# Four row pairs in a chain per feed-forward stage, and one weight sum of each pair made by accumulating DMAs

## What is computed

```
def swiglu(x, w13, w2):
    gate, up = jnp.split(x @ w13, 2, axis=-1)
    return (jax.nn.silu(gate) * up) @ w2
...
for i in range(DEPTH):
    x = layer_norm(ALPHA * x + 0.5 * swiglu(x, ffn1_w13[i], ffn1_w2[i]), ln_g[i, 0], ln_b[i, 0])
    ...
    x = layer_norm(ALPHA * x + 0.5 * swiglu(x, ffn2_w13[i], ffn2_w2[i]), ln_g[i, 2], ln_b[i, 2])
```

## Time and profile before

| | |
|---|---|
| median of 3 runs | 2465.41 us (2463.21 to 2465.69) |
| profiled execution | 2466.14 us, its span 2464.2 us |
| TensorE busy | 98% of the span, granted clock 0.996 |
| VectorE, ScalarE, GpSimd busy | 75%, 54%, 17% |
| HBM read | 414.92 MB, 169 GB/s over the span |

### The profile page before, as it was taken

One profiled execution on the slowest core, in us unless ns is written; L12 is line 12 of the kernel. 1 busy time (PEld: TensorE's weight loads), 2 busy tenths in 40 slices (PEclk: granted clock), 3 DMA queues, 4 the chain that ended last, 5 costly groups with the idle time before them and its releaser, 6 DMA issues. The chain is left out here.

```text
span 2464.2 us, 32871 instructions
## 1 busy us (share of the span) xinstructions
PE 2410.9 (98%) x13023; PEld 2027.1 (82%) x13023; DVE 1852.3 (75%) x2384; ACT 1319.6 (54%) x1637; POOL 409.4 (17%) x463
## 2 busy tenths in 40 slices
PE   9999999999999999999989999999999998999999
PEld 7888878888888888888878888888878876998998
DVE  5466679889875798898768888887675667897554
ACT  5444555555664556556556655664553355444442
POOL 0002310000001100000230000001359602580000
PEclk9999999999999999999999999999999999999999
DMA  8555445656554465565515565565445542336553
GB/s 273 188 187 156 143 146 190 204 171 200 193 172 137 137 197 196 177 199 188 167 58 184 188 209 171 187 206 158 133 149 191 189 153 71 116 124 205 171 188 111
DMA packets 313945, 418.10 MB, mean 170 GB/s; under 512 B 18761, under 2 KB 271042, under 8 KB 313794
## 3 DMA queue, kind: packets, MB, share of 16 engines
q1 hardware_dynamic: 313794, 416.01, 51.8%
HBM read 414.92 MB, written 1.05 MB: 169 GB/s over the span
## 5 line engine op out<-in xcount | busy, mean ns | idle before, releaser
L536 DVE TENSOR_TENSOR wlo<-raw,whi 128x2048 fp32r<-128x2048 f32 (+1 forms) x370 | 861.4, 2341 | 159.0 <-ACT whi L529 158.2
L529 ACT ACTIVATE whi<-raw 128x2048 fp32r<-128x2048 f32 (+1 forms) x375 | 700.4, 1887 | 6.0 <-DMA raw<-in_ffn_w_dram 3.1
L695 PE MATMUL ps<-whi,xh 128*128 128x512 f32 (+2 forms) x1367 | 510.8, 374 | 7.9 <-DVE wlo L1647 2.2
L697 PE MATMUL ps<-whi,xl 128*128 128x512 f32 (+2 forms) x1367 | 503.5, 368 | 0.0
L696 PE MATMUL ps<-wlo,xh 128*128 128x512 f32 (+2 forms) x1367 | 503.1, 368 | 0.0
L695 PE MATMUL ps<-whi,oh 128*128 128x512 f32 x944 | 380.1, 403 | 0.0
L697 PE MATMUL ps<-whi,ol 128*128 128x512 f32 x944 | 369.0, 391 | 0.0
L696 PE MATMUL ps<-wlo,oh 128*128 128x512 f32 x944 | 367.9, 390 | 0.0
L695 PEld LDWEIGHTS ps<-whi,xh 128*128 128x128 f32 x1367 | 258.0, 189 | 56.8 <-issue 11.9
L697 PEld LDWEIGHTS ps<-whi,xl 128*128 128x128 f32 x1367 | 257.9, 189 | 43.2
L696 PEld LDWEIGHTS ps<-wlo,xh 128*128 128x128 f32 x1367 | 258.2, 189 | 41.0
(11 more groups left out here) (412 smaller groups left out, 3988.8 us busy)
## 6 DMA issues: line engine op xcount, KB each, us to landing
raw<-in_ffn_w_dram SPq DMA_DIRECT2D x350, 512.0 KB, 4.9
raw<-in_ffn_w_dram SPq DMA_DIRECT2D x88, 1024.0 KB, 5.0
raw<-in_w_ff_dram SPq DMA_DIRECT2D x32, 1024.0 KB, 5.4
raw<-in_w_out_dram SPq DMA_DIRECT2D x20, 1024.0 KB, 4.9
raw<-in_w_in_dram SPq DMA_DIRECT2D x20, 1024.0 KB, 5.1
raw<-in_dsa_w_in_dram SPq DMA_DIRECT2D x32, 512.0 KB, 4.6
raw<-in_dsa_w_in_dram SPq DMA_DIRECT2D x12, 1024.0 KB, 5.1
raw<-in_fox_w_in_dram SPq DMA_DIRECT2D x16, 512.0 KB, 5.0
```

The lines of the kernel that those rows point to most:

```text
L529: act.activation(hi(u)[:, 0:w], raw[:, (slot[u] + 1) % SLOTS, 0:w], ACT.Copy).then_inc(sem("hi_ready"), n)
L536: dve.tensor_tensor(lo(u)[:, 0:w], raw[:, (slot[u] + 1) % SLOTS, 0:w], hi(u)[:, 0:w].bitcast(F32), ALU.subtract).then_inc(sem("lo_ready"), n)
L695: pe.matmul(o, ah, bh, start=start, stop=False, skip_group_check=True)
L697: return pe.matmul(o, al, bh, start=False, stop=stop, skip_group_check=True)
```

## The change

- `PAIRED` is (3, 5, 7, 9) and not (3, 6, 9): the stage has plain units 0, 1 and 2 and then four pairs, one behind the other.
- Where a pair follows a pair, the first two sums, their parts and the down splits are interleaved at the end of `paired`, in a new order on VectorE and ScalarE (`two_summed`, `three_summed`).
- The third form's sum is taken from VectorE. GpSimd issues two DMAs of 512 KB each that add the weights of unit v + 2, read from DRAM, onto raw(v + 1) in SBUF, once unit v + 1 has landed and form_1 is made. ScalarE's high part of the third form waits for both.
- In the last pair of a stage, VectorE splits one unit and not two ahead of the last `gated_low`.
- Room for descriptors of GpSimd's DMAs grows from 512 to 2048 bytes per partition; to make room, `cum`, `kr` and `rope_m` share the space of `BT`, which is used much later.

```diff
-PAIRED = (3, 6, 9)
+PAIRED = (3, 5, 7, 9)
...
+                if kind == "ffn":
+                    A, D = ffn_units(st)
+                    for n, q in enumerate(st["pairs"]):
+                        v = A(q + 1)
+                        dst = raw_of(v + 1).rearrange("p (k h c) -> p k h c", k=4, h=2)
+                        landed(pool, v + 1)
+                        pool.wait_ge(sem("form_made"), b("form_made", 0) + 3 * n + 1)
+                        for h in range(2):
+                            pool.dma_start(dst[:, :, h, :], units[v + 2][:, :, h, :], accum_op=ALU.add).then_inc(sem("third_form"), 16)
...
-                        act.wait_ge(sem("form_made"), b("form_made", 0) + 4 * n + f)
+                        if f == 3:
+                            act.wait_ge(sem("third_form"), b("third_form", 0) + 32 * n + 32)
+                        else:
+                            act.wait_ge(sem("form_made"), b("form_made", 0) + 3 * n + min(f, 3))
...
                         silu(q + 1, 1, ps[:, 5, 0:256])
+                        if q + 2 in pairs:
+                            split_hi(act, v + 6)
+                            gated_high(q)
+                            form_high(n + 1, 1, form_1h, form_1)
+                            form_high(n + 1, 2, form_2h, form_2)
+                            gated_high(q + 1)
+                            return
...
+                    def two_summed(q):
+
+                        v = A(q + 1)
                         landed(dve, v)
                         landed(dve, v + 1)
                         tt(form_1[:, :], raw_of(v + 1), raw_of(v), ALU.add).then_inc(sem("form_made"), 1)
+
+                    def three_summed(q):
+
+                        n, v = pairs.index(q), A(q + 1)
                         split_lo(dve, v)
                         landed(dve, v + 2)
-                        dve.wait_ge(sem("form_made"), made + 1)
+                        dve.wait_ge(sem("form_made"), b("form_made", 0) + 3 * n + 1)
                         tt(form_2[:, :], raw_of(v + 2), form_1[:, :], ALU.add).then_inc(sem("form_made"), 1)
...
-                        tt(raw_of(v + 1), raw_of(v + 2), raw_of(v + 1), ALU.add).then_inc(sem("form_made"), 1)
                         split_lo(dve, v + 2)
...
                         gate_rows(q + 1, 1, ps[:, 5, 256:512])
+                        if q + 2 in pairs:
+                            two_summed(q + 2)
+                            gated_low(q)
+                            three_summed(q + 2)
+                            form_low(n + 1, 1, form_1l, form_1, form_1h)
+                            gated_low(q + 1)
+                            form_low(n + 1, 2, form_2l, form_2, form_2h)
+                            return
                         gated_low(q)
-                        split_lo(dve, v + 7)
+                        split_lo(dve, v + 6 if q + 1 == FIT - 1 else v + 7)
                         gated_low(q + 1)
                         split_lo(dve, v + 8)
...
-    nc = _bacc.Bacc("TRN2", target_bir_lowering=False, num_devices=1, dynamic_dma_scratch_size=512)
+    nc = _bacc.Bacc("TRN2", target_bir_lowering=False, num_devices=1, dynamic_dma_scratch_size=2048)
```

More of the change, by code:

```diff
@@ L175, in stages_plan @@
             n = len(st["pairs"])
-            made.update(h0_done=FIT - 2 * n, rows_made=min(n, 1), rows_hi=min(n, 1), rows_lo=min(n, 1), form_made=4 * n, form_hi=4 * n,
+            made.update(h0_done=FIT - 2 * n, rows_made=min(n, 1), rows_hi=min(n, 1), rows_lo=min(n, 1), form_made=3 * n, third_form=32 * n, form_hi=4 * n,
                         form_lo=4 * n, form_used=3 * n, third_done=n, term_kept=4 * n, block_made=3 * n)
@@ L318, in build @@
         rt = sb("rt", [P, 4, 4 * 4 * 8])
-        cum = sb("cum", [P, S], F32R)
+        BT_at = nc.sbuf_base
+        BT = sb("BT", [P, 8, P])
+        cum = nc.alloc_sbuf_tensor_at("cum", [P, S], F32R, offset=BT_at)
         pick = sb("pick", [P, NH], F32R)
@@ L328, in build @@
         rope_p = sb("rope_p", [P, 2, 4, 8])
-        rope_m = sb("rope_m", [P, 2, NT, RP // 2])
+        rope_m = nc.alloc_sbuf_tensor_at("rope_m", [P, 2, NT, RP // 2], F32, offset=BT_at + 4 * S + 4 * NT * RP)
         upper = sb("upper", [P, NT, S])
@@ L351, in build @@
         bb = sb("bb", [P, 2, 16, 16])
-        BT = sb("BT", [P, 8, P])
         prm = sb("prm", [P, 20, 16])
         tick = sb("tick", [P, 1])
-        kr = sb("kr", [P, NT, RP])
+        kr = nc.alloc_sbuf_tensor_at("kr", [P, NT, RP], F32, offset=BT_at + 4 * S)
         form_1 = nc.alloc_sbuf_tensor_at("form_1", [P, W], F32, offset=heads_at)
@@ L1790, in row_lows @@
                         tt(rows_l[:, :, :, :], rows_s[:, :, :, :], rows_h[:, :, :, :].bitcast(F32), ALU.subtract).then_inc(sem("rows_lo"), 1)
-                    def before_pair(q):
-                        n, v, made = pairs.index(q), A(q + 1), b("form_made", 0) + 4 * pairs.index(q)
+                    def two_summed(q):
+                        v = A(q + 1)
                         landed(dve, v)
@@ L1797, in before_pair @@
                         tt(form_1[:, :], raw_of(v + 1), raw_of(v), ALU.add).then_inc(sem("form_made"), 1)
+                    def three_summed(q):
+                        n, v = pairs.index(q), A(q + 1)
                         split_lo(dve, v)
                         landed(dve, v + 2)
-                        dve.wait_ge(sem("form_made"), made + 1)
+                        dve.wait_ge(sem("form_made"), b("form_made", 0) + 3 * n + 1)
                         tt(form_2[:, :], raw_of(v + 2), form_1[:, :], ALU.add).then_inc(sem("form_made"), 1)
+                    def before_pair(q):
+                        n = pairs.index(q)
+                        two_summed(q)
+                        three_summed(q)
                         gate_rows(q - 1, 0, ps[:, 4, 256:512])
```

## The result

The changed kernel takes 2560.14 us (median, 2558.51 to 2565.28); the kernel before takes 2464.31 us on the same chip. The ratio is 1.039, with a 95% interval of 1.0377 to 1.0402: 3.9% slower, where 0.4% slower was forecast. It lies above the range, which ended at 2540. The profiled execution has a span of 2563.5 us where before had 2464.2, 99.3 us more, and a mean granted clock of 0.984 where before had 0.996.

What follows compares the result with a forecast made beforehand. TensorE, busy 98%, was taken as the bound, with VectorE nearly as full. Per stage -2.48 (pairing) + 3.45 (late `ol`) + 0.53 (stage end) = +1.50 us, six stages +9.0: forecast 2474.5 us, 0.37% slower, range 2461 to 2540.

Steps and rivals of the forecast that it cites:

- The accumulating DMAs: GpSimd's two transfers per pair: taken to overlap and need 9.8 us, under the 12.7 us allowed in a chain, costing nothing.
- The bounds of 4.9 and 19.6: Limits in us for the two transfers: one plain load's landing from below, one behind the other at half pace from above.
- The law of 18 us: Each microsecond of the transfers over 12.7 us costs three per stage, 18 us over six stages.
- The DMA is late: Rival, chance 0.24: the transfers take over 12.7 us, so ScalarE stands before the third form; 2480 to 2605 us.
- The sum ahead of `gated_low(q)`: On VectorE between chained pairs: makes `ol` late for TensorE's second down product, three times 1.15 us, +3.45 us per stage.
- The end of a stage: The wait for the last `ol` goes, but the moved split delays the norm and TensorE's transposes of `xn`; +0.53 us per stage.
- 72 matmuls, 14.9 us: One more pair per stage saves TensorE 12 products, 2.48 us per stage, 14.9 us over six stages.
- ScalarE at the third form 6.2 us after the pair's first matmul: ScalarE still makes the third form's high part 6.2 us after the pair's first matmul, given as a sign of being right.
- the sign given for the late DMA: A wait of ScalarE for a DMA at the third form, growing with each pair of a stage.
- VectorE slowed by descriptors: Rival, chance 0.04: GpSimd's descriptors lengthen two VectorE instructions per pair by 0.33 us each, at most 12 us; 2487 us.
- No stall: Rival, chance 0.12: VectorE reaches the last gate 1.15 us earlier, so the sum fits at pair transitions; 2454 us.
- half of it: Rival, chance 0.10: lag at the last gate some 3.7 us, stage end free, about -0.4 us per stage; 2463 us.

Runs made afterwards that it cites:

- experiments 1 and 6: The changed kernel with room for GpSimd's DMA descriptors of 2112 (2504.6 us) and of 3072 (2494.61 us, `bias` laid over BT) instead of 2048 bytes per partition.
- experiment 5: The changed kernel with ten matmuls of unread result ahead of TensorE's wait for the third form in each chained pair; 2543.62 us.
- experiment 2: The changed kernel with the third form's sum back on VectorE at the head of the pair and no accumulating DMAs; 2509.32 us.
- experiment 4: The changed kernel with `gated_low(q)` ahead of the next pair's first sum on VectorE; 2564.88 us.
- experiment 8: experiment 7 with VectorE's split at the end of a stage back where the kernel before had it; 2493.79 us.
- experiments 9 and 12: 9: experiment 8 with the next pair's first sum ahead of the split up to v + 5, 2460.65 us; 12: the same with descriptor room 2048, 2461.14 us.
- experiment 7: The changed kernel with descriptor room 3072 and `gated_low(q)` ahead of the next pair's first sum on VectorE; 2498.47 us.

## Why the prediction was wrong, point by point

**The accumulating DMAs: the step that failed.** The prediction took "9.8, the two overlapped and each at half the pace", under the 12.7 us allowed. Measured from the first sum: 15.4 to 19.3 us, 16.8 on average, since they did not overlap: the second was issued only when the first had landed, 6.5 us and more after it. The figure for two that overlap was near: without the wait for room it was 9.4 to 11.6 us in the same order on VectorE (experiments 1 and 6), and the time allowed was 13.0. So the step that failed is the overlap, not the pace. The bounds of 4.9 and 19.6 held. The law of 18 us for each microsecond over 12.7 was somewhat steep: 16.8 gives 74 us, the waits cost 58.5; 0.3 us of the difference per pair is the time allowed, and some 0.5 us is room between the third form's low part and TensorE's need of it (ScalarE waits 66.8 us, TensorE 55.6). The rival "The DMA is late" had the mechanism, with a chance of 0.24; the issue of the second DMA as an operation of its own, which can wait for room, was costed nowhere, though the rival names small scratch.

**A term that was missing: the clock.** Most waits of 2 us and more had 3 to 7 us at a granted clock of 0.50 about their end (14 of the 16 in the changed kernel). The prediction priced waits at their length only. That is up to 27 us of the 99 by the accounting, 17 to 26 by experiment 5. The prediction's sum with the waits as measured is 2474.4 + 58.5 + 3.7 + 0.7 = 2537, just inside the range; the clock put the time outside it. Waits of up to 1.6 us (experiment 2) cost no clock.

**The sum ahead of `gated_low(q)`: right.** 18 waits at the second down product, 21.5 us where some 21 were said, and 24.4 with 0.16 for each where the sum had 20.7. But in a kernel whose DMAs are late they cost nothing that taking them away would give back (experiment 4).

**The end of a stage: right.** L2537's wait is gone, the transposes of `xn` wait 1.57 us more per stage, +3.9 us in all where +3.2 were counted; the waits of experiment 8 give them back.

**72 matmuls, 14.9 us: right**, and in experiments 9 and 12 they show: 14.9 less 5.5 for the `ol` waits leaves 9.4, of which 4 to 5.5 are measured; where the rest goes is not known.

**ScalarE at the third form 6.2 us after the pair's first matmul: right only for a stage's first pair**, where 18.7 us are allowed; in the others it waits for the DMA, which was the sign given for the late DMA. In the first stage the wait is 2.86, 3.32 and 4.57 us. In each of the six stages the last is longer than the first, as the prediction's sign had it, though not always the second.

**VectorE slowed by descriptors: no.** 2.28 us beside the DMAs, as before. The chance of 0.04 was the author's estimate.

**No stall, and half of it: no.** The lag at the last gate was as said.

**What the prediction didn't see.** A chain of pairs makes VectorE the bound (34.4 us a pair with the sum, 32.2 without it in experiment 7's order, 31.6 with its idle 0.79 us filled; TensorE alone needs 31.1). The prediction noted "nearly as full as TensorE" and costed only the one late `ol`.

## What to carry to other kernels

Cost a transfer from the moment its data is ready to the moment its reader needs it, with the issue of each DMA as an operation of its own: two accumulating DMAs on GpSimd's queue may not go at once (in the changed kernel the second was issued 6.5 to 10.0 us after the first). Where a transfer is late by a little, moving its start a few microseconds up in the producer's order did more here (99 us, with two smaller moves) than more room for descriptors (56 to 66 us). A TensorE wait of over 2 us can cost more than its length, since in most cases here (14 of 16) the granted clock fell to 0.50 about it, for 3.4 or 6.8 us; those of up to 1.6 us in these stages cost no clock.

## What the runs showed of the hardware that was not expected

- Two accumulating DMAs of 512 KB from DRAM onto SBUF: 1.3 us of GpSimd for each issue; with room of 2048 the second was issued 6.5 to 10.0 us after the first, 0.3 us after that had landed; it was issued at once in two pairs of three with 2112 and in four of five with 3072. Landing takes 7.6 us (median) where a plain load takes 5.1.
- After TensorE stood 2.24 us it kept 0.23 us a matmul for 1.6 us and went to 0.43 us for some 3 us, at a granted clock of 0.50; two other waits, of 2.66 and 2.70 us, had nothing of the kind behind them. With ten matmuls whose result nobody reads in each wait, it came nowhere in these stages.
- A tensor_tensor of 128x2048 on GpSimd took 6.4 us and held VectorE's tensor_tensor (6.69 us in place of 2.28), which ended 2.15 us after it.
